# Two banks for turned probabilities, an earlier copy of the stream values, and places of their own for cached values in a two-layer streaming encoder

## The reference, cut to what matters

```python
h = rmsnorm(x)
proj = h @ w_in                          # one projection feeds all three branches
ya = fox(h)     # 6 heads of 64, softmax(q k / 8 + decay), causal, cached keys and values
yb = dsa(h)     # indexer: I[t,s] = sum_h w[t,h] relu(q_idx . k_idx); top-k keys; 4 heads of 64
yc = mla(h)     # 6 heads, low-rank q and kv latent, rotary key
x += (sigmoid(gate_a(h)) * (ya @ wo_a) + sigmoid(gate_b(h)) * (yb @ wo_b)
      + sigmoid(gate_c(h)) * (yc @ wo_c)) @ w_o
x += swiglu(rmsnorm(x))
```

## Time and profile before

| | us |
|---|---|
| median of 3 runs | 2155.23 (2154.59 to 2157.27) |
| the profiled execution, its own time | 2154.84 |
| its span | 2153.0 |
| PE busy | 2099.4 |
| DVE busy | 1392.0 |
| ACT busy | 968.7 |
| mean granted clock of PE, 1 is full | 0.998 |

### The profile page before, as it was taken

How to read it: one execution, slowest core, us unless ns; L and a number is a source line. 1 busy time by engine, 2 the same in 40 slices (tenths; PEclk the granted TensorE clock), 3 DMA queues, 4 the chain that set the end, 5 groups by cost and what they waited for, 6 DMA issues and landing times.

```text
span 2153.0 us, 36860 instructions
## 1 busy us (share of the span) xinstructions
PE 2099.4 (98%) x13616; PEld 1883.8 (87%) x13616; DVE 1392.0 (65%) x2833; ACT 968.7 (45%) x2056; POOL 395.1 (18%) x287
## 2 busy tenths in 40 slices
PE   9999999999999999999999999999999999999999
PEld 8998768878979989989899887787889899899897
DVE  4567875545839838838445678766367497396493
ACT  4236766556425424314232467665663353243241
POOL 1120020200004314314011200203000142242230
PEclk9999999999999999999999999999999999999999
DMA  6233224132332222222232332241423222222222
GB/s 217 78 106 127 83 83 124 59 112 104 119 106 79 79 79 80 88 79 89 77 137 76 110 114 88 79 133 55 149 76 135 72 92 86 79 79 88 72 96 79
DMA packets 90681, 207.83 MB, mean 97 GB/s; under 512 B 20676, under 2 KB 46920, under 8 KB 90184
## 3 DMA queue, kind: packets, MB, share of 16 engines
q1 hardware_dynamic: 90504, 205.48, 28.3%
HBM read 181.50 MB, written 23.95 MB: 95 GB/s over the span
## 4 chain that ended last, share of the span: by engine, by line
PE 89%; DVE 4%; ACT 3%; issue 2%; DVEq 1%; POOL 1%; DMA 1%; SPq 0%; ACTq 0%
PE ps L879 28%; PE ps L925 16%; PE ps L1404 8%; PE ps L1406 8%; PE ps L1405 8%; PE ps L937 6%; PE ps L1096 2%; PE ps L1116 2%; PE ps L995 1%; PE ps L1014 1%; PE ps L1040 1%; PE ps L1210 1%; PE ps L1384 1%; PE ps L1175 1%; POOL rsq L1939 1%
## 5 line engine op out<-in xcount | busy, mean ns | idle before, releaser
L1465 ACT ACTIVATE w_hi<-raw 128x1024 fp32r<-128x1024 f32 (+4 forms) x172 | 171.0, 997 | 398.4 <-PE ps L879 369.4
L1994 DVE TENSOR_TENSOR w_lo<-raw,w_hi 128x1024 fp32r<-128x1024 f32 (+4 forms) x124 | 139.1, 1123 | 187.7 <-ACT w_hi L1465 183.8
L925 PE MATMUL ps<-h_hi,w_hi 128*128 128x320 f32 x768 | 246.8, 321 | 1.5 <-ACT g L1465 1.5
L925 PE MATMUL ps<-h_hi,w_lo 128*128 128x320 f32 x768 | 237.7, 310 | 0.0
L925 PE MATMUL ps<-h_lo,w_hi 128*128 128x320 f32 x768 | 237.6, 309 | 0.0
L1404 PE MATMUL ps<-th_hi,op_hi 128*128 128x320 f32 x640 | 198.1, 310 | 3.8 <-issue 3.8
L1939 POOL TENSOR_TENSOR rsq<-ssq,mhalf 128x12 f32<-128x12 f32 (+3 forms) x56 | 118.0, 2107 | 447.7 <-DVE ssq L2072 385.1
L1406 PE MATMUL ps<-th_hi,op_lo 128*128 128x320 f32 x640 | 198.2, 310 | 0.0
L1405 PE MATMUL ps<-th_lo,op_hi 128*128 128x320 f32 x640 | 198.0, 309 | 0.0
L879 PE MATMUL ps<-w_hi,act_hi 128*128 128x512 f32 x440 | 174.5, 397 | 0.0
L879 PE MATMUL ps<-w_lo,act_hi 128*128 128x512 f32 x440 | 174.4, 396 | 0.0
(11 more groups left out here) (376 smaller groups left out, 5327.5 us busy)
## 6 DMA issues: line engine op xcount, KB each, us to landing
raw<-in_weights SPq DMA_DIRECT2D x212, 512.0 KB, 3.3
gates<-gst SPq DMA_DIRECT2D x72, 160.0 KB, 1.8
g<-gates SPq DMA_DIRECT2D x12, 960.0 KB, 7.0
raw<-in_weights SPq DMA_DIRECT2D x24, 384.0 KB, 3.0
ktb<-in_cache_fox_kt SPq DMA_DIRECT2D x16, 384.0 KB, 4.8
vc<-in_cache_fox_v SPq DMA_DIRECT2D x16, 384.0 KB, 4.1
x_sb<-in_x_prompt SPq DMA_DIRECT2D x8, 512.0 KB, 4.6
out_y_prompt<-x_sb SPq DMA_DIRECT2D x8, 512.0 KB, 3.4
```

The lines of the kernel that those rows point to most:

```text
L925: mm = pe.matmul(ps[:, 5, 0:HALF], w[:, kk * P:(kk + 1) * P], h_pair[x][:, kk, half * HALF:(half + 1) * HALF], start=kk == 0 and n == 0, s ...
L1465: return act.activation(dst, src, ACT.Copy, scale=scale)
L1994: dve.tensor_tensor(low[:, 0:width], raw[raw_slot(c)][:, 0:width], high[:, 0:width].bitcast(F32), ALU.subtract).then_inc(lo_made.sem, 1)
```

## The change

Five things are edited.

1. The four jobs `("dsa", 2)` and `("gate_sums", 0)`, at the end of the projection, use banks 3 and 4 and not 6 and 7. The first index scores wait for them.
2. `turn(i)` uses bank 7 when the item before it used bank 3, i is at least 4, and no side job of step i + 2 uses bank 7 (items 7, 11, 15, 19, 30, 32, 34 and on); otherwise bank 3. It waits for the copy of the last item that was turned in its bank (`TURN_PRIOR`), and in bank 7 for the last job there too (`TURN_JOB`); a side job in bank 7 waits for the last turn there (`JOB_TURN`).
3. On ACT, `outputs` of stream items (fewer than 128 rows) come one step earlier, between `turned_out` and `exp`. In steps with an `index_turn`, `gate_move` comes behind the copies of the side jobs.
4. The cached fox values have four places: `vc2` where `wqb` was, `vc3` where `vc2` was. Streams 5, 6 and 7 use `vc2`, `vc3` and `vc1`.
5. At the end of the attention DVE makes the high part of `at_dsa` as well as the low part, for columns 0 to 511 once the dsa streams begin to be copied out, and for the last 128 columns when all jobs are copied out.

```diff
--- before.py
+++ after.py
@@ -187,11 +187,23 @@
     JOBS += _jobs
 
 THIRD = [JOB["mla_turn", _t] + 2 for _t in range(TT)]
+EARLY = {JOB[_p] + _k: 3 + _k for _p in (("dsa", 2), ("gate_sums", 0)) for _k in range(2)}
 BANK, PRIOR, _used = [], [], {}
 for _j in range(JOBS):
-    BANK.append(5 if _j in THIRD else 6 + (_j - sum(_k < _j for _k in THIRD)) % 2)
+    BANK.append(5 if _j in THIRD else EARLY[_j] if _j in EARLY else 6 + (_j - sum(_k < _j for _k in THIRD)) % 2)
     PRIOR.append(_used.get(BANK[_j], -1))
     _used[BANK[_j]] = _j
+
+
+STEP_OF = {JOB[_part] + _k: _n for _n, _side in enumerate(SIDE) for _part in _side if _part in JOB
+           for _k in range(3 if _part == ("mla_expand", TT - 1) else _JOBS_OF[_part[0]])}
+_side_steps = {_step for _j, _step in STEP_OF.items() if BANK[_j] == 7}
+TURN_BANK, TURN_PRIOR, TURN_JOB = [], [], []
+for _n in range(N_ITEMS):
+    TURN_BANK.append(7 if _n >= 4 and TURN_BANK[-1] == 3 and _n + 2 not in _side_steps else 3)
+    TURN_PRIOR.append(1 + max([_m for _m in range(_n) if TURN_BANK[_m] == TURN_BANK[_n]], default=-1))
+    TURN_JOB.append(1 + max([_j for _j in range(JOBS) if BANK[_j] == 7 and STEP_OF.get(_j, -1) < _n + 2]) if TURN_BANK[_n] == 7 else 0)
+JOB_TURN = [1 + max([_n for _n in range(N_ITEMS) if TURN_BANK[_n] == BANK[_j] and _n + 2 < STEP_OF.get(_j, -1)], default=-1) for _j in range(JOBS)]
 
 
 PEN_AT = {1: 0, 2: 256, 3: 640}
@@ -389,7 +401,7 @@
         gate_past = [home(f"gate_past{k}", [120, PAST], BF16) for k in range(2)]
         cum_new = home("cum_new", [102, P])
         gate_new = home("gate_new", [102, P], BF16)
-        vc = [home(f"vc{k}", [P, 2, FH * HD], F32, "vc", 3072 * k) for k in range(2)] + [home("vc2", [P, 2, FH * HD], F32, "bias")]
+        vc = [home(f"vc{k}", [P, 2, FH * HD], F32, "vc", 3072 * k) for k in range(2)] + [home("vc2", [P, 2, FH * HD], F32, "wqb"), home("vc3", [P, 2, FH * HD], F32, "bias")]
 
 
         kpe = home("kpe", [P, TT, ROPE])
@@ -481,7 +493,7 @@
         g_done, g_moved, g_out = (sig("g_done", GATE_HALVES // 2), sig("g_moved", GATE_HALVES),
                                   [sig(f"g_out{k}", 16 * 3 * GATE_KEPT) for k in range(2)])
         g_in, g_ready, acc_made, mix_half = sig("g_in", 16 * GATE_KEPT), sig("g_ready", KD), sig("acc_made", KD), sig("mix_half", KD)
-        at_hi, at_lo, vd_made = sig("at_hi", 1), sig("at_lo", 3), sig("vd_made", 1)
+        at_lo, vd_made = sig("at_lo", 3), sig("vd_made", 1)
         rows_free = sig("rows_free", 2)
         plain_made, plain_high = sig("plain_made", FF_PLAIN), sig("plain_high", FF_PLAIN)
         silu_ready, act_ready = sig("silu_ready", DFF // P, 2), sig("act_ready", DFF // P, 2)
@@ -495,7 +507,7 @@
         lf_abs, lf_log = sig("lf_abs", 1), sig("lf_log", 3)
         lfr_made, grow_made = sig("lfr_made", 1), sig("grow_made", 1)
 
-        vc_in = [sig(f"vc_in{k}", 16 * (DECB // 2 - k)) for k in range(2)] + [sig("vc_in2", 16)]
+        vc_in = [sig(f"vc_in{k}", 16 * n) for k, n in enumerate((3, 3, 1, 1))]
         ktb_in, ctb_in = ([sig(f"{n}{k}", 16 * DECB // 4) for k in range(4)] for n in ("ktb_in", "ctb_in"))
         rope_in, rope_high, rope_split = sig("rope_in", 16), sig("rope_high", 2), sig("rope_split", 2)
         ckvc_in, cn_made = sig("ckvc_in", 16), sig("cn_made", 1)
@@ -720,12 +732,20 @@
                         sp.wait_ge(it_scores.sem, it_scores.at(L, I_FOXS + b - 3))
                         own_wait(sp, sp_tick)
                         fox_keys(b)
+                    if step == I_FOXS + 5:
+                        sp.wait_ge(tp_done.sem, tp_done.at(L, JOB["mla_expand", TT - 1] + 3))
+                        own_wait(sp, sp_tick)
+                        sp.dma_start(vc[2][:, :, :], past("fox_v", 5)).then_inc(vc_in[2].sem, 16)
                     if step == I_FOXS + 7:
                         sp.wait_ge(tp_done.sem, tp_done.at(L, JOB["mla_turn", TT - 1] + 4))
                         own_wait(sp, sp_tick)
-                        sp.dma_start(vc[2][:, :, :], past("fox_v", DECB - 1)).then_inc(vc_in[2].sem, 16)
+                        sp.dma_start(vc[3][:, :, :], past("fox_v", 6)).then_inc(vc_in[3].sem, 16)
+                    if step == I_FOXS + 8:
+                        sp.wait_ge(it_pv.sem, it_pv.at(L, I_FOXS + 4))
+                        own_wait(sp, sp_tick)
+                        sp.dma_start(vc[1][:, :, :], past("fox_v", 7)).then_inc(vc_in[1].sem, 16)
                     b = step - (I_FOXS + 2)
-                    if 2 <= b < DECB - 1:
+                    if 2 <= b < 5:
 
                         sp.wait_ge(it_pv.sem, it_pv.at(L, I_FOXS + b - 1))
                         own_wait(sp, sp_tick)
@@ -977,6 +997,8 @@
 
                     if PRIOR[j] >= 0:
                         pe.wait_ge(tp_out.sem, tp_out.at(L, PRIOR[j] + 1))
+                    if JOB_TURN[j]:
+                        pe.wait_ge(it_pt.sem, it_pt.at(L, JOB_TURN[j]))
                     if j in THIRD:
                         pe.wait_ge(g_moved.sem, g_moved.at(L, gates_begun[0]))
                         beside_gates.append(j)
@@ -1088,12 +1110,15 @@
                         pe.wait_ge(it_norm.sem, it_norm.at(L, NORMED[i + 1]))
                     else:
                         pe.wait_ge(it_exp.sem, it_exp.at(L, i + 1))
-                    if i:
-                        pe.wait_ge(it_pt.sem, it_pt.at(L, i))
+                    bank = TURN_BANK[i]
+                    if TURN_PRIOR[i]:
+                        pe.wait_ge(it_pt.sem, it_pt.at(L, TURN_PRIOR[i]))
+                    if TURN_JOB[i]:
+                        pe.wait_ge(tp_out.sem, tp_out.at(L, TURN_JOB[i]))
                     if rows < 96:
                         own_wait(pe, pe_tick)
                     for j in range(blocks):
-                        last = pe.transpose(ps[:, 3, j * P:j * P + rows], probs[0:rows, i % 3, j * P:(j + 1) * P],
+                        last = pe.transpose(ps[:, bank, j * P:j * P + rows], probs[0:rows, i % 3, j * P:(j + 1) * P],
                                             cst("ident", 0, rows, rows))
                     last.then_inc(it_tr.sem, 1)
 
@@ -1125,8 +1150,8 @@
                         return
                     s, pt = t % 2, probs_t[:, PT_AT[i]:PT_END[i]]
                     if kind == "foxs":
-                        s = 2 if t == DECB - 1 else s
-                        pe.wait_ge(vc_in[s].sem, vc_in[s].at(L, 16 * (t // 2 + 1) if s < 2 else 16))
+                        s = (0, 1, 0, 1, 0, 2, 3, 1)[t]
+                        pe.wait_ge(vc_in[s].sem, vc_in[s].at(L, 16 * (1, 1, 2, 2, 3, 1, 1, 3)[t]))
                     if i == I_MLAS:
                         pe.wait_ge(cn_made.sem, cn_made.at(L, 1))
                         pe.wait_ge(ckvc_in.sem, ckvc_in.at(L, 16))
@@ -1267,6 +1292,7 @@
                 def index_scores(i):
 
                     if i == 0:
+                        pe.wait_ge(tp_out.sem, tp_out.at(L, JOB["gate_sums", 0] + 2))
                         pe.wait_ge(zi_ready.sem, zi_ready.at(L, 1))
                         pe.wait_ge(iktb_in.sem, iktb_in.at(L, 16))
                         pe.wait_ge(proj_out.sem, proj_out.at(L, TT * len(GROUPS)))
@@ -1587,7 +1613,7 @@
                     if PT_FREE[i]:
                         act.wait_ge(it_pv.sem, it_pv.at(L, PT_FREE[i]))
                     view = lambda a: a.rearrange("p (j r) -> p j r", r=P)[:, :, 0:rows]
-                    copy(view(probs_t[:, PT_AT[i]:PT_END[i]]), view(ps[:, 3, 0:blocks * P])).then_inc(it_pt.sem, 1)
+                    copy(view(probs_t[:, PT_AT[i]:PT_END[i]]), view(ps[:, TURN_BANK[i], 0:blocks * P])).then_inc(it_pt.sem, 1)
 
                 def normalise(i):
                     _, _, _, rows, blocks, width = item_shape(i)
@@ -1754,22 +1780,26 @@
                         act.wait_ge(store_mla.sem, store_mla.at(L, 2 * STORED))
                     if 1 <= step <= N_ITEMS:
                         normalise(step - 1)
-                    if 4 <= step < N_ITEMS + 4:
+                    if 4 <= step < N_ITEMS + 4 and item_shape(step - 4)[3] == P:
                         outputs(step - 4)
-                    if step:
-                        for k in GATES_IN[step - 1]:
-                            if k != GATE_LAST:
-                                gate_move(k)
+                    moves = [k for k in GATES_IN[step - 1] if k != GATE_LAST] if step else []
+                    turning = any(kind == "index_turn" for kind, n in SIDE[step])
+                    if not turning:
+                        for k in moves:
+                            gate_move(k)
                     if step == N_ITEMS + 2:
                         gate_move(GATE_LAST)
                     for kind, n in SIDE[step]:
                         beside(kind, n)
+                    if turning:
+                        for k in moves:
+                            gate_move(k)
                     if 2 <= step < N_ITEMS + 2:
                         turned_out(step - 2)
```

(15 more changed lines are left out.)

## The result

The changed kernel takes 2131.43 us (median of 4 runs, 2128.58 to 2132.40), against 2154.91 us for the kernel before (4 runs, 2152.53 to 2157.27). The ratio is 0.9889 with a 95% interval of 0.9872 to 0.9906: about 24 us less. The forecast was 2136, its range 2127 to 2147. The profiled execution took 2130.57 us, its span 2128.8. The mean granted clock listed with the four executions is 1.000 (2128.58 us), 0.999 (2130.57) and 0.998 (2132.29 and 2132.40). So much of what parts them is how often the clock fell, and the median lies between an execution with few falls and one with more. The kernel before took 2150.68 us in the one execution on record that is listed at 1.000, which is 22.1 above the changed kernel's 2128.58.

The account below looks back on a forecast made before the run. TensorE, 98% busy, was taken to bound the kernel, so only its idle time could be gained. Gains of 23.5 us less 5.0 for the index steps left 18.5 off 2154.84: 2136 us, range 2127 to 2147.

Parts of the forecast that it names:

- part 2: Fox streams, more places for cached values: load waits go (3.3 us) and the clock stays up (3.2), 6.5 us gained.
- parts 1, 3, 4 and 5: Gains from early jobs (3.5 us), probability transposes (7.0), stream values (4.8) and the high part at the attention's end (1.7).
- part 1: Projection's end, four early jobs in banks 3 and 4: PE's waits for qtd and grow copies go, 3.5 us gained.
- part 6: Index steps, ACT's new copy order: ACT idles for index-query transposes and later copies come late, 5.0 us lost.
- part 4: Streams, values copied ahead of the exponentials: PE's waits for av go, 4.8 us gained.
- rival C: Fox streams: the clock falls after 321 in each layer all the same, 3.2 us less gain, 2139 us; chance 0.09.
- Part 3: Probability transposes in banks 3 and 7 by turns: waits for ACT's probs_t go, 7.0 us gained.
- Rival A: Freed waits of transposes and stream values only move to the next copy; 11.8 us of gain lost, 2148 us; chance 0.18.
- rival D: Streams: ACT's exponential, held behind the values, makes the next scores late; 43 us lost, 2179 us; chance 0.05.
- Rival B: Index steps: the reorder costs nothing, as ACT's later copies find slack; 2129 us; chance 0.12.

Follow-up runs that it names:

- e2: Changed kernel with all turns of the 24 fox items in bank 3, ACT's changed order kept: 2129.46 us against 2131.43.
- e6: Changed kernel with ACT's copies of the stream values back in their old place, at the start of the next step: 2139.97 us against 2131.43.
- e9: Changed kernel with the cached fox values in three places and their loads in the old order again: 2136.45 us against 2131.43.
- e4: Changed kernel with the gate's copies parted in every step: gate half first, weight's high part last, ahead of the exponential: 2129.89 us against 2131.43.
- e3: Changed kernel with the old order of the gate's copies and bank 3 for the 24 fox items: 2126.52 us against 2131.43.
- e13: As e10, but the gate weight's high part comes behind the exponential in all steps: 2141.59 us.
- e1: Changed kernel with ACT's gate copy and w_hi ahead of the side jobs' copies again in the index steps, banks as changed: 2126.59 us against 2131.43.
- e11: Changed kernel with the high part of at_dsa made by ACT in one copy again, DVE's subtraction behind it: 2132.55 us against 2131.43.
- e10: As e2, but in index steps ACT does the gate's copy first and the weight's high part after the other copies, before the exponential: 2124.09 us.
- e12: As e10, but in the index steps the gate weight's high part comes behind the exponential: 2128.83 us.

## Why the prediction was right

The mechanism of each part held, with a reservation on part 2, and the result lies in the range: 18.5 us forecast for the profiled execution, 24.3 measured. What was off is the size of the gains. Those of parts 1, 3, 4 and 5 all came out above the upper bounds that the prediction gave them (3.5, 8.1, 5.7 and 1.7).

**A wait is worth more than its row.** Parts 1, 3, 4 and 5 were priced by the listed idle time. By position they gave 5.3, 8.7, 6.6 and 2.3 us against 3.5, 7.0, 4.8 and 1.7. Part of that are waits that are not in the sum: one of 0.24 us per layer in part 1 (L1244, for `qtd`), which I overlooked, and half of the dsa streams' (0.9), which I held back and which did not come back at all. The rest is a surplus on each wait. Four waits of 1.97 us in all gave 2.65, and four of 2.86 in the mla items gave 3.56, so 0.17 us each above what is listed. In the streams it is less: three waits of 2.12 us in the mla streams of layer 0 gave 2.45, three of 0.88 in the dsa streams 1.01. The scores' last matmul and the transposes behind it, in the kernel before (whose second row is in the earlier trace rows, at 375.83) and in the one after, show where it comes from:

```profile
374.56 0.22 PE L1041 MATMUL ps<-masks 128*128 128x128 bf16 x1
...
368.73 0.22 PE L1063 MATMUL ps<-masks 128*128 128x128 bf16 x1
368.79 0.60 PE L1121 MATMUL ps<-consts,probs 128*128 128x128 f32 x4
```

Before, 375.83 - 374.56 = 1.27 us lay between the two starts, and the wait is listed as 1.05, from the end of the first. After, it is 368.79 - 368.73 = 0.06: the transposes start while the matmul ahead of them still runs, 0.16 us before its modelled end. The gain is 1.21, the wait and the overlap that it had prevented. Such surpluses and the clock make up the fall of 7.4 us in PE's busy time: 4.6 us above the listed waits in parts 1, 3, 4 and 5, and 3.0 in part 2's stretch (6.4 less 3.3), less 0.2 in part 6.

**Part 6, the cost, was right in size and place.** Forecast, step by step, -0.26, 0, +0.43, +0.48, +0.12, +0.54, +0.50, +0.23, +0.50; the positions of the gate halves give -0.34, +0.04, +0.45, +0.43, +0.15, +0.55, +0.44, +0.25 and +0.40. It could be worked out since it is a chain of durations that all stood in the timeline. I put too much of it to bank 7, though: at the shared scores the wait is 0.26, and e2 gives 0.6 us per layer to the bank where I had nearly 1.0.

**Part 2** came out at 6.4 against 6.5, but its working was only half right, and the close match is partly luck. The loads landed in time and the clock stayed up, as forecast. (The 0.25 in its sum has no row in the prediction; it is the rest of stream 6's values, 0.65 us at the low clock and 0.40 at the full one.) But 2.8 of the 6.4 us need part 4 too (e6), which the sum did not know. That the clock's share is certain, as the sum had it, is refuted by e9; the 3.2 us were there to be gained because the clock had fallen in both layers of the one profile before. By the rule from the Trainium skill that I weighed ("TensorE: Matmul & The Clock Gate", Part 1: The HAM clock gate) the clock follows what PE did of late, and the changed kernel agrees with it: the same thin matmuls without the wait run at 1.00 (rival C is out). No run here tells why one layer of e9 fell and the other did not.

**Part 3** gave more than was counted (8.7 against 7.0), and the place that I held back behaved as said: the wait of 0.56 at 483.75 went, and came back at the gate behind it,

```profile
478.06 0.41 PE L945 MATMUL ps<-h_hi,w_hi 128*128 128x320 f32 x1 [0.85 <-ACT g L1491]
```

which is 0.85 us where the earlier trace rows had 0.27. By position the gain there was 0.6 us and was lost again within five us. Rival A describes this one place and no other.

**Part 4**: rival D, the exponential held behind the values, is not seen in the changed kernel. The exponential waits for DVE in the mla streams as before, and e6, which undoes it, is slower. e4, which holds the exponentials one high part longer, gains 2.3 us less than e3 in layer 0, but its new waits are for copies, and e13, which holds no exponential, is slower still. So neither shows D's mechanism. Rival B (nothing paid for the index order) falls by e1. Its time, 2129, was nearer to the result than mine, for another reason.

## What to carry to other kernels

Price a freed wait of TensorE by the distance between the two starts, not by the idle time listed: each gave 0.17 us more here in the transposes, and 0.04 to 0.11 in the streams. Where two versions lie within a few us, compare executions with the same mean granted clock, or positions in the two timelines, before the medians: e11's 2 us and the right size of e10's gain show only there. In a queue that works in order, put the short copy that another engine needs now ahead of a long one that is needed steps later, but look at both ends: the copy that must wait for its input does not go ahead of one that is ready, and the long one must not slip behind the moment at which the next engine makes its own link of a chain. Undoing one part at a time overstates and understates: a wait may hide another, as the late load seems to have hidden the late `av`.

## What was not expected of the hardware

The granted clock falls behind some of PE's waits and not behind others of the same length. The fourteen profiles, from 15 us on, have 42 waits of PE of 1.55 to 2.41 us. Behind 22 of them the clock fell to 0.50, at the latest 1.7 us behind the wait's end, for three to over six us; behind 20 it stayed at 1.00. It never fell behind a shorter wait: not behind 1.10 and 0.81 us close together (e9, layer 1), and not behind any other of the 129 waits of 0.8 to 1.5 us. It fell behind 1.72 and 1.61 us (the kernel before), 1.66 (e9, layer 0), 1.55 (e1) and 1.83 (e13, both layers), but behind none of the four waits of 1.60 us of e4 and e10. Behind the same wait in the feed-forward part (L1430 in the changed kernel, 1.78 to 2.26 us) it fell 15 times of 28. The clearest case is e12, where the wait for `sq_a` (L1205) is as long in both layers, and the clock fell in layer 0 (0.50 in the window shown above) but not in layer 1. PE's row and a window of layer 1, then the wait and a window in the feed-forward part of the changed kernel:

```profile
1317.93 1.56 PE L1205 MATMUL ps<-wkv,ct 128*128 128x384 f32 x4 [2.41 <-ACT sq_a L1672]
...
1320.00:1323.00 3.00, 2.98 (x27) 2.16 (x27) 2.81 (x11) 2.44 (x7) 1.47 (x1) 1.00 0.19 65
...
676.62 0.39 PE L1430 MATMUL ps<-th_hi,op_hi 128*128 128x320 f32 x1 [1.91 <-issue]
...
677.00:680.00 3.00, 3.00 (x14) 3.00 (x13) 2.02 (x5) 0.06 (x1) 1.53 (x1) 0.50 0.00 0
```

A fall cost 1.3 to 2.8 us more than the wait itself (1.3 in e1, 2.8 in e9), and 0.2 in e12, where PE's next waits were shorter for it. So such a wait can cost twice its row or more where the clock falls, and about its row where it does not. The length of the wait alone does not decide it, and what does no run here shows.
